# Where a two-block kernel prepares its state-space coefficients, saves its residual, and how fast it steps through the state-space pairs

## The reference, cut to what matters

```
x = x + ssd_layer(...)            # its last matmul is o_w_out ("oo" in the kernel)
h = rmsnorm(x, final_norm)        # the residual of the second block ("nx")
proj = rmsnorm_2(h, norm_mix) @ w_in      # u, q, k, v, r, a, q', k', v', gates
y_a = s5_branch(u, ...)           # 64 groups of 16 channels, 64 complex states each
y_b = gla_branch(...); y_c = diff_attn_branch(...)
h = h + (g0*y_a + g1*y_b + g2*y_c) @ w_out    # needs h again ("wo")
```

## Time and profile before

| | |
|---|---|
| median of 3 runs | 3216.24 us (3215.72 to 3217.17) |
| profiled execution, its time | 3217.17 us |
| its span, first to last instruction | 3215.4 us |
| granted TensorE clock, mean | 0.988 |
| busy: PE, DVE, ACT, POOL | 3089.6, 2301.2, 1830.6, 532.8 us |

### The profile page before, as it was taken

How to read it: one execution, slowest core, us unless ns; L and a number is a source line. 1 busy time by engine, 2 the same in 40 slices (tenths; PEclk the granted TensorE clock), 3 DMA queues, 4 the chain that set the end, 5 groups by cost and what they waited for, 6 DMA issues and landing times.

```text
span 3215.4 us, 53602 instructions
## 1 busy us (share of the span) xinstructions
PE 3089.6 (96%) x21726; PEld 2853.5 (89%) x21726; DVE 2301.2 (72%) x3156; ACT 1830.6 (57%) x2363; POOL 532.8 (17%) x640
## 2 busy tenths in 40 slices
PE   7999898999999999999988999999999999999998
PEld 6889888889999999889877899999998888888886
DVE  6655788657778877675866787786656888888544
ACT  5554677645666676645556454444445666666443
POOL 2000000000000000114743565760001000000000
PEclk9999999999999999999999999999999999999999
DMA  5445434556555555556433444456555555555554
GB/s 198 141 155 179 142 133 142 198 191 217 181 174 184 178 177 201 192 177 208 156 115 112 142 153 157 170 173 210 184 184 190 190 190 190 190 190 190 190 190 138
DMA packets 158473, 560.50 MB, mean 174 GB/s; under 512 B 17600, under 2 KB 25856, under 8 KB 157712
## 3 DMA queue, kind: packets, MB, share of 16 engines
q1 hardware_dynamic: 158224, 557.06, 51.8%
HBM read 550.64 MB, written 6.36 MB: 173 GB/s over the span
## 4 chain that ended last, share of the span: by engine, by line
PE 67%; DVE 17%; ACT 10%; issue 3%; POOL 2%; DMA 0%; SPq 0%; DVEq 0%; ACTq 0%; POOLq 0%
PE ps L565 67%; DVE WL L1336 5%; ACT WH L912 3%; ACT L902 3%; DVE XV L1310 2%; DVE YB L1310 1%; ACT DB L902 1%; DVE XV L1306 1%; DVE YS L1299 1%; DVE DB L1299 1%; ACT RS L902 1%; DVE XP L1299 0%; POOL PB L1922 0%; DVE ZB L1299 0%; DVE XC L1310 0%
## 5 line engine op out<-in xcount | busy, mean ns | idle before, releaser
L565 PE MATMUL ps<-XN,WH 128*128 128x256 f32 (+1 forms) x8864 | 1855.8, 303 | 34.2 <-DVE XN L1310 17.7
L912 ACT ACTIVATE WH<-RAW 128x1024 fp32r<-128x1024 f32 x1010 | 1064.9, 1058 | 1119.7 <-PE ps L565 1078.9
L1336 DVE TENSOR_TENSOR WL<-RAW,WH 128x1024 fp32r<-128x1024 f32 x1010 | 1259.6, 1253 | 444.8 <-ACT WH L912 439.3
L565 PEld LDWEIGHTS ps<-XN,WH 128*128 128x128 f32 x8864 | 1434.2, 192 | 112.9 <-DVE XN L1310 18.6
L565 PE MATMUL ps<-XN,WL 128*128 128x256 f32 x5120 | 1444.5, 282 | 0.0
L565 PEld LDWEIGHTS ps<-XN,WL 128*128 128x128 f32 x5120 | 980.9, 192 | 0.0
L565 PE MATMUL ps<-YS,WH 128*128 128x512 f32 (+1 forms) x1088 | 372.9, 390 | 9.7 <-DVE WL L1336 5.1
L565 PE MATMUL ps<-YS,WL 128*128 128x256 f32 x1056 | 297.3, 281 | 0.0
L1922 POOL TENSOR_TENSOR RSB<-RSB,SQ 128x256 f32<-128x256 f32 x75 | 75.9, 1012 | 1224.7 <-ACT SQ L902 1223.5
L565 PEld LDWEIGHTS ps<-YS,WH 128*128 128x128 f32 x1088 | 204.5, 190 | 55.3 <-DVE WL L1336 6.7
L565 PE MATMUL ps<-HS,WH 128*128 128x512 f32 x688 | 238.6, 392 | 0.0
(11 more groups left out here) (332 smaller groups left out, 3347.2 us busy)
## 6 DMA issues: line engine op xcount, KB each, us to landing
RAW<-in_w SPq DMA_DIRECT2D x1010, 512.0 KB, 3.4
CSB<-sums SPq DMA_DIRECT2D x64, 128.0 KB, 3.8
X<-scratch SPq DMA_DIRECT2D x2, 2048.0 KB, 8.2
X<-in_x SPq DMA_DIRECT2D x4, 512.0 KB, 8.3
X<-in_x SPq DMA_DIRECT2D x1, 2048.0 KB, 8.0
scratch<-X SPq DMA_DIRECT2D x1, 2048.0 KB, 8.6
scratch<-X SPq DMA_DIRECT2D x4, 512.0 KB, 5.4
out<-X SPq DMA_DIRECT2D x4, 512.0 KB, 2.6
```

The source lines that it names most:

```text
L565: return pe.e.matmul(dst, l, r, start=start, stop=stop, skip_group_check=True)
L912: act.e.activation(WH[:, w % NH, :], RAW[:, w % NB, :], ACT.Copy).then_inc(*act.one(("wh", w)))
L1336: dve.e.tensor_tensor(WL[:, w % NB, :], RAW[:, w % NB, :], WH[:, w % NH, :].bitcast(F32), SUB).then_inc(*dve.one(("wl", w)))
```

## The change

The coefficients (`s5c`) move from the `oo` stage to the `u` stage, with seven steps instead of eight; the final norm (`nx`) moves from the g0 stage to the `u` stage, ahead of the store; the residual is stored once, already normed, and u(2)'s evacuation waits for the store; the S5 chain starts behind u(7) instead of u(0), at ten borders a pair instead of twelve. Some tiles get other places in SBUF.

```diff
-    "s5c": 8, ... "s5": 207, "wo": 1,
+    "s5c": 7, ... "s5": 178, "wo": 1,
...
-    oo = out_proj("oo", "o_w_out", list(range(28)), list(range(28, 32)), "ys2", [End("ssd", (7,)), Now("s5l", ())])
-    p += oo[:12] + [Now("st2", (0,)), Go("s5c", ())] + oo[12:16] + [Now("st2", (1,))] + oo[16:20] + [Now("st2", (2,))]
-    p += oo[20:]
+    p += out_proj("oo", "o_w_out", list(range(28)), list(range(28, 32)), "ys2", [End("ssd", (7,))])
...
     p += [Part(u[0], list(range(15)), True, False), Now("nend", (2,)), Now("nend2", ()), Part(u[0], [15], False, True)]
-    p += [Now("st2", (3,)), Now("wg", ()), Now("ring3", ()), Go("s5", ())]
+    p += [Now("s5l", ()), Go("nx", ()), Go("s5c", ())]
     for j in range(1, 8):
         if j == 2:
-            p.append(Now("rst", ()))
+            p += [End("nx", ()), Now("st2", ()), Now("rst", ())]
         p.append(whole(u[j], 16))
+    p += [End("s5c", ()), Now("ring3", ()), Now("wg", ()), Go("s5", ())]
...
-        if n == 4:
-            p.append(Go("nx", ()))
...
-    p += [End("nx", ()), Now("ring4", ())]
+    p.append(Now("ring4", ()))
...
+        P1 = [m(f"P1{i}", 32) for i in range(10)]
+        PW = m("PW", 2 * 8 * 32).rearrange("p (c l a) -> p c l a", c=2, l=8)
         ZS = v3(Map(nc, m.at, end)("ZS", 8 * 512, F32R), 8)
...
-        m = Map(nc, ys2_end, c0)
-        CRR, CIR, C1 = [v3(m(n, 1024), 32) for n in ("CRR", "CIR", "C1")]
-        C2 = flat(US)[:, 0:1024].rearrange("p (a b) -> p a b", a=32)
+        m = Map(nc, r1, r2)
+        CRR, CIR = v3(m("CRR", 1024), 32), v3(m("CIR", 1024), 32)
+        C1, C2 = v3(m("C1", 1024), 32), v3(m("C2", 1024), 32)
...
             def u(j, s):
+                if j == 2:
+                    dve.wait_ge(*at("st2"))
                 evac(US[:, j, :], 2, "u", j, more=[("us", j)])
...
             def s5(s):
                 if s == 0:
                     pool.wait_ge(*at("pw"))
-                    pool.wait_ge(*at("st2"))
-                    pool.wait_ge(*at("rs", 2))
...
-                m, r = divmod(s - 4, 12)
+                m, r = divmod(s - 4, 10)
...
             def s5l():
-                sp.wait_ge(*at("yz", 7))
+                sp.wait_ge(*at("rs", 2))
+                load(BR, args["b_re"], "b1")
+                load(BI, args["b_im"], "b2")
                 load(CRR, args["c_re"], "c1")
                 load(CIR, args["c_im"], "c2")
...
-            def st2(q):
-                sp.wait_ge(*at("xa", 2, 4 * q + 3))
-                load(scratch[:, 4 * q:4 * q + 4, :], X[:, 4 * q:4 * q + 4, :], "st2")
+            def st2():
+                sp.wait_ge(*at("nx", 3))
+                load(scratch, X, "st2")
...
-    return [(m, s - 8 - 12 * m) for m in range(16) if 0 <= s - 8 - 12 * m < 13]
+    return [(m, s - 9 - 10 * m) for m in range(16) if 0 <= s - 9 - 10 * m < 13]
```

More of the change, by code:

```diff
@@ L420, in build @@
         YS2 = v3(m("YS2", 32 * 512, F32R), 32)
-        ys2_end = m.at
         CST = m("CST", 128)
@@ L454, in build @@
         BI = v3(m("BI", 8 * 128), 8)
-        P1 = [m(f"P1{i}", 32) for i in range(10)]
-        PW = m("PW", 2 * 8 * 32).rearrange("p (c l a) -> p c l a", c=2, l=8)
-        c0 = m.at
         CR = v3(m("CR", 32 * 32), 32)
@@ L515, in build @@
         out_done = sem("out_done")
-        marks = {n: (s, 64 if n == "st2" else 16) for n, s in dma_in.items()}
+        marks = {n: (s, 16) for n, s in dma_in.items()}
         where = {}
@@ L1127, in s5c @@
                 if s == 0:
-                    act.wait_ge(*at("y2", 7))
+                    act.wait_ge(*at("tile", "u", 0))
                     fn(dt, cv("log_dt", 0, 32), ACT.Exp, ("sdt",))
@@ L1219, in s5 @@
                         act.wait_ge(*at("bu", n))
-                        act.wait_ge(*at("st2"))
                         if n > 1:
@@ L1225, in s5 @@
                         fn(BS[i][:, 1, :], b[:, 0:256], ACT.Copy, ("bx", n), ("free", "bu", n), scale=-1.0)
-                if s == 202:
+                if s == 173:
                     act.wait_ge(*at("usd", 7))
                     fn(US, US, ACT.Gelu_apprx_tanh, ("gelu",))
-                if s == 204:
+                if s == 175:
                     fn(ZS[:, :, 0:256], US, ACT.Copy, ("zsh",))
@@ L1630, in nx @@
             def nx(s):
-                dve.wait_ge(*at("x3"))
                 for k in range(4 * s, 4 * s + 4):
@@ L1680, in s5c @@
                     tt(fi_, c1, den, MUL)
-                frb, fib = [x.unsqueeze(2).to_broadcast([128, 32, 32]) for x in (fr_, fi_)]
                 if s == 6:
@@ L1684, in s5c @@
                     dve.wait_ge(*at("c2"))
+                    frb, fib = [x.unsqueeze(2).to_broadcast([128, 32, 32]) for x in (fr_, fi_)]
                     tt(C1, CRR, frb, MUL)
@@ L1687, in s5c @@
                     tt(CR, C1, C2, SUB)
-                if s == 7:
                     tt(C1, CRR, fib, MUL)
@@ L1712, in dec @@
                     stt(GE1, GE1, 0.0, GE2, MIN, SUB)
-                    dve.wait_ge(*at("st2"))
                     scan(CUM, cs("creset"), GE1, 0.0, MUL, ADD)
@@ L1823, in s5 @@
                             ("free", "sy", ft))
-                if s == 206:
+                if s == 177:
                     dve.wait_ge(*at("zsh"))
@@ L2058, in s5l @@
             def s5l():
-                sp.wait_ge(*at("yz", 7))
+                sp.wait_ge(*at("rs", 2))
+                load(BR, args["b_re"], "b1")
+                load(BI, args["b_im"], "b2")
                 load(CRR, args["c_re"], "c1")
                 load(CIR, args["c_im"], "c2")
-            def st2(q):
-                sp.wait_ge(*at("xa", 2, 4 * q + 3))
-                load(scratch[:, 4 * q:4 * q + 4, :], X[:, 4 * q:4 * q + 4, :], "st2")
+            def st2():
+                sp.wait_ge(*at("nx", 3))
+                load(scratch, X, "st2")
             def wg():
-                sp.wait_ge(*at("rs", 2))
                 sp.wait_ge(*at("cc"))
-                load(BR, args["b_re"], "b1")
-                load(BI, args["b_im"], "b2")
                 load(WG, args["w_gate"], "wg")
```

## The result

| | before | after |
|---|---|---|
| median | 3216.7 us (3215.72 to 3218.85, 4 runs) | 3238.16 us (3237.38 to 3239.43, 4 runs) |
| ratio | | 1.0073, 95% interval 1.0060 to 1.0084 |
| span of the profiled execution | 3215.4 us | 3236.5 us |

The changed kernel is slower by 21.5 us. The forecast was 3226 us, slower by 10, with a range of 3212 to 3240; the direction was right and 3238.16 lies inside the range, near its end, but the size was half of what came. What was wrong was one term of the sum. The windows of the changed kernel are cut at the same units as those of before: length, busy time (instructions) of PE, PEld, DVE, ACT, POOL, then clock and DMA.

The account below looks back on a forecast made before the run. PE was taken to set the pace, with DVE costing time only through late deliveries. The terms -8.5 + 22.7 + 0 - 4.2 + 0 gave +10.0 on 3217.17, 3227.2; with the median 0.9 lower, 3226 us, range 3212 to 3240.

Parts of the forecast that it names:

- oo loses 8.5 us: Units 415 to 418: without the coefficients' burst on DVE, 19.60 us become 11.08; 3.3 of the 8.5 are clock.
- The u stage, +22.7: Norm, store wait and coefficients queue on DVE: PE 21.0 us late at unit 459, plus 1.7 of clock.
- The store's wait: In the u stage, DVE idles 6.0 us before u(2) until the store lands, 8.6 us after its issue.
- Step 6: New step 6 of the coefficients on DVE in the u stage, former steps 6 and 7 together: 8.4 us.
- the 1.5 us weighed for POOL: Possible extra in the u stage if DVE's step 6 and WL run slower beside POOL's table; not in the sum.
- nx out of g0, 0: g0 stage: the norm covered itself where PE was busy 132.62 of 132.62 us, so removing it gives nothing back.
- The late start, -4.2: S5 starts 14 borders later, so DVE's wait for TB goes: 2.4 us of PE's wait for u(7), 1.8 of clock.
- g12, 0: Pairs denser in g12: POOL's cycle must fall from 36.7 to 31.0 us and should just hold; no time change.
- The gla and diff stages, "0, between -12 and +8": Up to unit 572, denser pairs cost +4, the `lam` wait gives -6; the -2 was taken as 0.
- one known meeting (`lam`), -6: PE's 8.6 us wait at 1727 for `lam`'s product P shrinks: -4.4, and -1.7 for one fall of the clock.
- The rival in which the later stages give time back: Gla and diff waits, partly coincidence of 12-border pairs with 24-border chains, break at ten borders: 3214 us, no change; chance 0.20.
- the waits behind 1557 changing by over 12 us: Sign that the forecast is wrong: waits from the gla and diff stages on change by more than 12 us.

Follow-up runs that it names:

- the run with the four loads later: Changed kernel with the final norm back in g0, the residual stored un-normed after oo, and loads BR, BI, CRR, CIR two borders later; ratio 1.0027.

## Why the prediction was right and wrong

**oo loses 8.5 us: right.** 19.60 became 11.09 us, and the spread coefficients gave the same from the other side. The price of the slower clock behind the two waits, 0.83 over 19.60 us, was part of it.

**The u stage, +22.7: right, 22.6.** The order written out by hand and priced by single rows held to a microsecond over 48. That 22.6 meets 22.7 so closely is in part luck: PE was 20.1 us late at unit 459 where 21.0 were written, and 2.5 came behind it where 1.7 were. The store's wait was 4.8 instead of 6.0. Step 6, whose six operations ran beside POOL's table, took 8.1 us (1512.42 to 1520.50) where 8.4 were taken, and of the WL only the last was long, 1.64 us; so the 1.5 us weighed for POOL didn't come. SP's own wait for nx cost nothing, as said. With the store earlier and the four loads right behind it RAW came late, which the sum did not contain; with the loads two borders later it held again, 7.1 for 7. That it held in the changed kernel, where loads and store are 13 us apart, is likely owed to that distance.

**nx out of g0, 0: right**: 132.62 and 132.64 us.

**The late start, -4.2: nearly right, -5.8.** The wait for TB went. The rest is side matmuls of the first pair, which moved behind unit 472 (PE has 154 instructions here instead of 165).

**g12, 0: right in time, wrong in its parts.** PE was idle 3.0 us there (255.66 - 252.67), where it had none, and one pair's side matmuls fewer made up for it. POOL's cycle is 30.8 and 31.9 us from start to start of TB's copy, where 31.0 was needed:

```profile
2017.32 0.52 POOL L1975 COPY TB<-PB 128x64 f32<-128x64 f32 x1
...
2048.09 0.25 POOL L1975 COPY TB<-PB 128x64 f32<-128x64 f32 x1
...
2080.02 0.51 POOL L1975 COPY TB<-PB 128x64 f32<-128x64 f32 x1
```

**The gla and diff stages, "0, between -12 and +8": wrong, +15.4.** This is the step that failed. It treated S5's work there as a load: it took half of a fifth, +4, and set one known meeting (`lam`), -6, against it, which did go, and gave 12.1 us. It looked only for waits of the old order that the new one would lose, and put those that the new order would make, outside the half of a fifth, at nothing. The runs show that the number of pairs is not the measure: the old density in another phase costs 415 to 419 us. Nor is DVE's time for them without price, since the new density with little of it takes 384; what counts is what that time falls upon. The clock was mis-sized with it: 0.03 x 397 = 12 us were written down for today's loss, half of 20.5 us is 10, and it became at most 22 where the forecast had let it grow by a tenth. And the tenth pair's side matmuls, some 4 us that moved into this stretch, were in no term.

In the kernel before a pair recurs every 12 borders and the chains of gla and diff every 24, so all pairs meet them at the same few places, and in that phase the stretch cost 397 to 401. With three borders more it cost 415 to 419. One border earlier, with `lam` moved too, it was 390 to 391, against 396 with `lam` moved alone, and most of that difference is the clock of single executions. At ten borders a pair meets the chains at ever other places; six of the ten stages (the table's seven, 472 to 487, 544 to 559 and 560 to 571) lost 31 us together and the others gave back 15. Two phases at ten borders were run, 412.8 and 418.4; whether a better one exists is not known. The rival in which the later stages give time back had the mechanism, and the sign against it. The bounds should have come from the phase: three borders, which leave the density as it is, moved the stretch by 14 and 22 us, so a bound of some 20 us to either side would have been fair. Nothing in the trace of the kernel before alone gives that figure.

What stays open: which single chains make the 5 us differences between phases was read from the names of waits (GE, BS, ST, SQ) and not tested one by one; nor were DVE's and POOL's parts told apart.

## What to carry to other kernels

When an engine is late by a queue, write its instructions down in order with their single prices from the timeline: that gives the lateness to a microsecond. When work recurs in a rhythm beside other chains in the same in-order engines, its share of busy time says little; shifting it by three borders moved 14 and 22 us here, by four 5.6, and by one no more than the executions scatter, so try phases before anything else is built on one. Where a burst stands beside borders with idle time, spreading it can be worth more than moving it: spread inside the oo stage the coefficients gave 8.5 us back; moved to the u stage they gave the oo stage the same 8.5 and cost the u stage 10.0 (58.9 against 48.9, the run with the four loads later).

## Not expected

Of the 15.4 us in the stretch from unit 472 PE's idle time shows only 2.2; the slower clock makes some 9, so a reader of busy shares alone would miss most of it. The prediction's own sign for this, the waits behind 1557 changing by over 12 us, would not have shown it either. And stages repeat to 0.05 us between different kernels (412.80 and 412.84) as long as the clock falls alike, and differ by 5 us where it doesn't, while units 0 to 221, where nothing differs, scatter by 3.0 us (745.1 to 748.1) from trace to trace.
